# A triangular inverse's second merge level from 32-column products without a mask, and the next k evacuated and convolved ahead of v's last tanh and SiLU

## Time and profile before

| what | value |
|---|---|
| median of 3 runs | 1137.81 us (1136.37 to 1139.96) |
| the profiled execution's own time | 1139.61 us |
| its span, first to last instruction | 1137.9 us |
| TensorE busy | 1072.2 us (94%) |
| VectorE busy | 780.1 us (69%) |
| ScalarE busy | 509.7 us (45%) |
| GpSimd busy | 524.0 us (46%) |
| DMA, share of 16 engines | 27.2% |

### The profile page before, as it was taken

One profiled execution on the slowest core, in us unless ns is written; L12 is line 12 of the kernel. 1 busy time (PEld: TensorE's weight loads), 2 busy tenths in 40 slices (PEclk: granted clock), 3 DMA queues, 4 the chain that ended last, 5 costly groups with the idle time before them and its releaser, 6 DMA issues.

```text
span 1137.9 us, 18866 instructions
## 1 busy us (share of the span) xinstructions
PE 1072.2 (94%) x5372; PEld 876.3 (77%) x5372; DVE 780.1 (69%) x1664; ACT 509.7 (45%) x1262; POOL 524.0 (46%) x753
## 2 busy tenths in 40 slices
PE   3897799999999999999999999999999999999984
PEld 2766588878888888888888888888888888887863
DVE  4678585785858586685858586695758586695835
ACT  3663434444344434444354434435354444435333
POOL 2242544555344643546344653546343653446413
PEclk9898999999999999999999999999999999999988
DMA  9922231223121331223221231223221221213103
GB/s 316 305 87 68 66 78 49 58 57 98 46 66 39 83 77 47 57 58 88 55 66 39 74 84 40 66 58 84 59 60 45 74 73 52 66 58 84 31 28 129
DMA packets 142054, 87.29 MB, mean 77 GB/s; under 512 B 21254, under 2 KB 136616, under 8 KB 141992
## 3 DMA queue, kind: packets, MB, share of 16 engines
q1 hardware_dynamic: 141992, 86.68, 27.2%
HBM read 77.76 MB, written 8.91 MB: 76 GB/s over the span
## 4 chain that ended last, share of the span: by engine, by line
PE 79%; DVE 11%; issue 4%; ACT 2%; DMA 1%; POOL 1%; SPq 0%; DVEq 0%; ACTq 0%; POOLq 0%
PE bank L415 37%; PE bank L517 16%; DVE work L967 3%; PE bank L561 2%; PE bank L549 2%; PE bank L571 2%; PE bank L553 2%; PE bank L574 2%; PE bank L490 2%; DVE y L990 2%; PE bank L599 2%; PE bank L476 1%; PE bank L430 1%; PE bank L463 1%; PE bank L437 1%
## 5 line engine op out<-in xcount | busy, mean ns | idle before, releaser
L1377 POOL TENSOR_TENSOR w_lo<-w_raw,w_hi 128x256 fp32r<-128x256 f32 x384 | 304.9, 825 | 280.2 <-ACT w_hi L696 270.5
L415 PE MATMUL bank<-h_hi,w_hi 128*128 128x512 f32 x760 | 327.4, 431 | 4.6 <-ACT w_hi L696 4.6
L415 PE MATMUL bank<-h_lo,w_hi 128*128 128x512 f32 x760 | 300.6, 396 | 0.0
L415 PE MATMUL bank<-h_hi,w_lo 128*128 128x512 f32 x760 | 203.2, 399 | 0.0
L967 DVE SCALAR_TENSOR_TENSOR work<-pre,cw,work 128x512 f32<-128x512 f32 x192 | 164.2, 855 | 13.3 <-ACT work L723 4.8
L415 PEld LDWEIGHTS bank<-h_hi,w_hi 128*128 128x128 f32 x760 | 144.0, 190 | 34.6 <-ACT w_hi L696 5.3
L415 PEld LDWEIGHTS bank<-h_hi,w_lo 128*128 128x128 f32 x760 | 142.6, 188 | 30.2
L415 PEld LDWEIGHTS bank<-h_lo,w_hi 128*128 128x128 f32 x760 | 144.2, 190 | 27.4 <-issue 0.5
L1420 POOL TENSOR_TENSOR og_lo<-work,og_hi 128x256 fp32r<-128x256 f32 x64 | 47.3, 739 | 217.1 <-ACT og_hi L778 217.1
L737 ACT ACTIVATE work<-work 128x512 f32<-128x512 f32 x64 | 40.3, 629 | 219.1 <-DVE work L967 208.1
L517 PE MATMUL bank<-wo_hi,og_hi 128*128 128x512 f32 x256 | 113.3, 443 | 7.1 <-DVE y L990 7.1
(11 more groups left out here) (175 smaller groups left out, 1745.5 us busy)
## 6 DMA issues: line engine op xcount, KB each, us to landing
w_raw<-in_gdn_w_in SPq DMA_DIRECT2D x96, 512.0 KB, 4.0
work<-in_ada_w SPq DMA_DIRECT2D x8, 1024.0 KB, 9.6
w_raw<-in_gdn_w_out SPq DMA_DIRECT2D x16, 512.0 KB, 3.4
y<-in_x SPq DMA_DIRECT2D x8, 512.0 KB, 9.3
work<-in_ada_w SPq DMA_DIRECT2D x8, 512.0 KB, 5.2
n_dram<-work SPq DMA_DIRECT2D x16, 256.0 KB, 2.3
out<-y SPq DMA_DIRECT2D x8, 512.0 KB, 2.6
work<-in_ada_b SPq DMA_DIRECT2D x1, 512.0 KB, 5.4
```

The costliest lines, as they stand in the source:

```text
L415: mm = nc.tensor.matmul(bank[m % 2][:, :], w[:, m % 2, k, :], h[:, k, half, :], start=(r == 0), stop=(r == MM - 1))
L1377: i = nc.gpsimd.tensor_tensor(w_lo[:, k % 2, j:j + 2, :], w_raw_k[:, k % 2, j:j + 2, :], w_hi[:, k % 2, j:j + 2, :].bitcast(F32), ALU.subt ...
```

## The change

The second merge level (`lv == 1`) takes only the blocks that are wanted. `merge_p` makes, for each chunk and each b in (0, 64), a product of 32 stationary columns against 32 moving ones, written to partitions b+32 to b+64. `merge_p_out` copies that into `pm` with two plain copies of 32 partitions, with no mask; `merge_d` likewise makes two products of 32 by 32 columns per chunk; `merge_d_out` subtracts with two instructions. The mask tile loses its middle level. `turn_k` and `decay_exponents` move from behind level 1 to behind level 2's first product. On ScalarE k's evacuation moves ahead of v's last tanh, and on VectorE v's last SiLU moves behind k's convolution.

```
-        pair_mask = sb("pair_mask", [P, 3, P])
+        pair_mask = sb("pair_mask", [P, 2, P])
...
-                    if lv < 2:
+                    if lv == 0:
                         mm = nc.tensor.matmul(p_bank[:, c, :, :], nmat[:, c, :], pairs(tm, lv)[:, c, :, 0, :],
                                               start=True, stop=True)
+                    elif lv == 1:
+                        for b in (0, 64):
+                            mm = nc.tensor.matmul(bank[5][b + 32:b + 64, DV + c * 32:DV + (c + 1) * 32],
+                                                  nmat[:, c, b + 32:b + 64], tm[:, c, b:b + 32], start=True, stop=True)
...
-                    if lv < 2:
+                    if lv == 0:
                         mm = nc.tensor.matmul(halves(bank[4], lv)[:, c, :, :], pm[:, lv, c, :], u_odd,
                                               start=True, stop=True)
+                    elif lv == 1:
+                        for b in (0, 64):
+                            mm = nc.tensor.matmul(bank[4][b:b + 32, c * 32:(c + 1) * 32], pm[:, lv, c, b:b + 32],
+                                                  u_fin[:, c, b + 32:b + 64], start=True, stop=True)
...
                 for lv in range(3):
                     merge_p(u, lv)
+                    if lv == 2 and not last:
+                        turn_k(u + 1, 1 - par)
+                        decay_exponents(u + 1)
                     fill(in_merge[lv][0])
                     merge_d(u, lv)
                     fill(in_merge[lv][1])
-                    if lv == 1 and not last:
-                        turn_k(u + 1, 1 - par)
-                        decay_exponents(u + 1)
...
+                if not last:
+                    evacuate(u, par, hd + par, 0)
                 tanh(u - 1, 5, 3, cvv[:, 1, :])
...
                 else:
-                    evacuate(u, par, hd + par, 0)
...
+                if lv == 1:
+                    for b in (0, 64):
+                        i = nc.vector.tensor_copy(pm[b + 32:b + 64, lv, :, b:b + 32],
+                                                  bank[5][b + 32:b + 64, DV:DV + NCH * 32].rearrange(
+                                                      "p (c w) -> p c w", c=NCH))
+                    i.then_inc(S["merge_p_out"], 1)
+                    return
...
+                        for b in (0, 64):
+                            u_odd = u_fin[b:b + 32, :, b + 32:b + 64]
+                            i = nc.vector.tensor_tensor(u_odd, u_odd, bank[4][b:b + 32, 0:NCH * 32].rearrange(
+                                "p (c w) -> p c w", c=NCH), ALU.subtract)
...
                 merge_p_out(u, 1)
-                silu(u - 1, 5, cvv[:, 1, :])
                 if first:
                     gate_wo(hd, 0)
                 if not last:
                     conv(u, par, nxt, 0)
+                silu(u - 1, 5, cvv[:, 1, :])
...
-            for lv in range(3):
+            for lv in (0, 2):
```

More of the change, by code:

```diff
@@ L1058, in merge_p_out @@
                 passed(dve, "merge_p", u, lv + 1)
+                if lv == 1:
[5 more added lines that the diff above has]
+                    return
                 p_out = (pairs(pm[:, lv, :, :], lv)[:, :, :, 0, :] if lv < 2
                          else pm_last.rearrange("p c (b w) -> p c b w", w=w))
-                mask = pair_mask[:, lv, :].rearrange("p (b q w) -> p b q w", q=2, w=w)[:, :, 0, :]
+                mask = pair_mask[:, lv // 2, :].rearrange("p (b q w) -> p b q w", q=2, w=w)[:, :, 0, :]
                 nc.vector.tensor_tensor(p_out, halves(bank[5], lv, (lv % 2) * DV),
@@ L1068, in merge_d_out @@
                 if lv < 2:
-                    u_odd = pairs(u_fin, lv)[:, :, :, 1, :]
-                    nc.vector.tensor_tensor(u_odd, u_odd, halves(bank[4], lv), ALU.subtract
-                                            ).then_inc(S["u_merged"], 1)
+                    if lv == 0:
+                        u_odd = pairs(u_fin, lv)[:, :, :, 1, :]
+                        i = nc.vector.tensor_tensor(u_odd, u_odd, halves(bank[4], lv), ALU.subtract)
+                    else:
+                        for b in (0, 64):
+                            u_odd = u_fin[b:b + 32, :, b + 32:b + 64]
+                            i = nc.vector.tensor_tensor(u_odd, u_odd, bank[4][b:b + 32, 0:NCH * 32].rearrange(
+                                "p (c w) -> p c w", c=NCH), ALU.subtract)
+                    i.then_inc(S["u_merged"], 1)
                     passed(dve, "u_merged", u, lv + 1)
@@ L1344, in _ @@
             select(after[:, :], [[-1, P]], -1, 1, ALU.is_ge, 0.0)
-            for lv in range(3):
+            for lv in (0, 2):
                 s = BLK << lv
                 n = P // (2 * s)
-                m = pair_mask[:, lv, :].rearrange("p (b q w) -> p b q w", q=2, w=s)[:, :, 0, :]
+                m = pair_mask[:, lv // 2, :].rearrange("p (b q w) -> p b q w", q=2, w=s)[:, :, 0, :]
                 then(nc.gpsimd.memset(m, 1.0))
```

## The result

| | before | after |
|---|---|---|
| median, us | 1137.92 (4 runs, 1136.37 to 1139.96) | 1124.05 (4 runs, 1122.74 to 1125.45) |
| ratio, 95% interval | | 0.9877 [0.9855, 0.9899] |
| the profiled execution, own time / span | 1139.61 / 1137.9 | 1122.74 / 1120.9 |

The change makes the kernel 13.9 us faster.

What follows compares the result with a forecast made beforehand. TensorE, busy 94% of the span, was taken to bound the kernel, with its waits for VectorE. Blocks -2.2, seven waits -2.9 and unit 0 -0.8 gave -5.9 us: 1132, range 1127 to 1146.5.

Steps and rivals of the forecast that it cites:

- the bounds of the narrow block: Level 1 block on TensorE, before 0.90 us: upper 1.24 (+10.9 in all), lower 0.58 (-10.2), middle 0.83 taken (-2.2).
- Rival C: Level 1's two column groups overlap, 16 instructions costing what 8 do: -13.9 us, 1123.9; chance 0.07.
- rival D: Level 1 blocks: every change of column group pays the fixed 0.33 us again, +74 us, about 1206; chance 0.05.
- A: Level 1 blocks slower: narrow products no faster than 0.057 us each, +7.2 us with the waits, 1145.0; chance 0.15.
- The 1.32 us: Level 1 block priced from the skill page's bound of about 62 ns per matmul; +13 us on these blocks alone.
- The seven waits: Transpose of k waiting 0.42 us for VectorE's SiLU in units 2, 4, ... 14; moving turn_k removes them, -2.9 us.
- the slack of 0.44: Unit 2: level 1's transpose ends 0.44 us before level 2's first product would start, so no wait there.
- same 0.42 us before another line in even units: Sign that the forecast is wrong: even units' 0.42 us wait on TensorE stands before a different line.
- VectorE's two for one: Level 1 on VectorE: two copies and two subtractions replace one each, +0.3 us a unit, at most +0.8.
- Unit 0, -0.8 us: Level 2's first product goes into TensorE's wait for VectorE's chain in unit 0, saving 0.8 us.
- k_gram: ScalarE's exponential stays early enough for k_gram: cover falls from 1.93 to 1.1 us, without a wait.

Runs made afterwards that it cites:

- e3_groups_in_turn: Changed kernel with the same 16 instructions per level 1 block, all of one column group first, then all of the other: 1127.87 us, ratio 0.9921.
- e5_turn_k_only: Changed products with turn_k and decay exponents moved behind level 2's first product, ScalarE and VectorE in the order of the kernel before: 1127.86 us, ratio 0.9916.

## Why the prediction was wrong

**The step that failed is the choice between the bounds of the narrow block.** I took 0.33 + 16 x 0.031 = 0.83 us "since the pace halved exactly when the columns did", -2.2 us in all. Measured is 0.57, the lower bound's 0.58: 0.33 less a block, and 0.33 x 32 = 10.6 us. The pace of one group was right, 0.032 between neighbours in `e3_groups_in_turn`, and so was the fixed 0.33. What I missed is that 16 instructions alternating between two groups are two streams of eight. No row before held two column groups, and I read that as evidence against overlap ("no row shows any overlap of blocks"), where it is none for either side. Rival C had the mechanism and the price of a block and a chance of 0.07. A page that I had read for rival D says it: TensorEngine Tiling of the Trainium skill, section Key Properties, that different tiles can load weights and multiply in parallel. The trace after agrees, with loads 0.015 us apart. I used only that section's sentence on draining. That rival C's sum, 1123.9, is met to 0.2 us is in part luck: it has 2 x 0.32 + 0.42 = 1.06 us in an even unit and 0.64 in an odd one, and the traces have 0.78 and 0.93.

**Rivals A and D.** Both are excluded. The block costs 0.57; A wanted 1.24, D some 2.3 more. The 1.32 us that I had estimated for a block is excluded too. That a change of group doesn't drain the engine is shown by seven changes in a block of 0.57 us.

**The seven waits, -2.9 us.** With the old products this was right: the order alone loses them and gives 5.1 us instead of 3.7. The extra is in two places. 0.14 us an even unit lies between level 1 and the Gram matrix and I can't assign it further. 0.19 an odd unit is a wait that I had not counted, level 0's second product behind VectorE's masked copy. L490's idle time for that copy was 3.3 us in 7 waits before and 1.9 in 6 with the order alone. In the changed kernel it is this, at L494:

```profile
  DVE pm L1078: 1.9, 6
```

In the changed kernel itself the waits did not go but moved. TensorE comes to level 2's first product 0.67 us sooner, and the slack of 0.44 that I had worked out is used up. In an even unit this product starts 0.29 us later behind level 1 than in an odd one, and the transpose of k behind it another 0.19 later, since it still waits for the SiLU: 0.48 us, as much as even units lost before (9.36 - 8.88 in the table, and 8.87 - 8.39 after). That is the "same 0.42 us before another line in even units" of my last sentence. In unit 2 (TensorE, then VectorE):

```profile
246.67 1.98 PE L415 MATMUL bank<-h_hi,w_lo 128*128 128x512 f32 x8
248.88 0.68 PE L483 MATMUL bank<-work 128*64 128x64 f32 x8 [0.23 <-DVE work L1098]
249.68 0.65 PE L424 MATMUL bank<-ident,work 128*128 128x128 f32 x4
```

```profile
242.75 0.59 DVE L1070 COPY pm<-bank 32x128 f32<-32x128 f32 x2
243.37 2.77 DVE L976 SCALAR_TENSOR_TENSOR work<-pre,cw,work 128x512 f32<-128x512 f32 x3
246.06 0.68 DVE L983 SCALAR_TENSOR_TENSOR work<-work 128x512 f32<-128x512 f32 x1
246.66 1.22 DVE L1043 TENSOR_TENSOR w_raw<-w_raw,gate_bc 128x1024 f32<-128x1024 f32 x1
247.91 0.57 DVE L1091 TENSOR_TENSOR work<-work,bank 32x128 f32<-32x128 f32 x2
248.52 0.30 DVE L1098 STREAM_TRANSPOSE work<-work 32x128 f32<-32x128 f32 x1
248.85 0.69 DVE L983 SCALAR_TENSOR_TENSOR work<-work 128x512 f32<-128x512 f32 x1
```

From 242.75 to 248.82 VectorE has no gap to speak of, and L483 starts 0.06 later. The SiLU ends at 249.54 and the transpose of k starts at 249.68, 0.80 behind L483; in unit 5 it is 440.11 - 439.50 = 0.61. The convolution follows the copies at once, as I had said; the earlier trace rows had the wait between.

**The sum as a sum.** I added the blocks and the waits. The two runs of a part each show that they don't add: with the blocks alone all 10.6 us turn into waits for VectorE, since in every unit the time that TensorE can come earlier without waiting (the cover) is shorter than the gain. The move of turn_k puts level 2's first product, about 0.8 us, ahead of it in each unit. `e5_turn_k_only` shows that this move by itself brings back 10.4 us.

**VectorE's two for one.** I took +0.3 us a unit. The copies and the next instruction start 0.62 apart (242.75 to 243.37), the subtractions and the transpose 0.61 (247.91 to 248.52). Before, one masked copy took 0.34 and one subtraction 0.44 from start to start, so it is +0.45 us.

**Unit 0, -0.8 us.** It is 1.13 us shorter with both parts. How much of that is the order can't be told: the products alone make it 0.04 us shorter, at the same granted clock over the unit (0.95), and the trace of the order alone, 0.50 us longer, has it at 0.89. So no run shows the -0.8 by itself. Level 2's first product did go ahead of the transpose of k, but it started only at the end of the wait, 3.77 us of it, when level 1's transpose was done; the SiLU cost another 0.28. The clock over 124 to 128 us was the same as in the earlier trace rows:

```profile
124.00:128.00 4.00, 4.00 (x17) 2.34 (x17) 0.53 (x2) 2.75 (x13) 3.97 (x7) 0.60 0.01 2
```

**k_gram.** No wait came back there. TensorE has no idle time before it in the trace, and from the transpose of k to it are 4.01 us in even and odd units alike.

## What to carry to other kernels

Before adding a saving on the busiest engine to the sum, ask at the next wait on that engine how much earlier it may come; where the other engine's chain is the longer one, the saving is zero, and a piece of independent work moved in between can be worth as much as the saving (10.4 of 10.6 us here). Small products that write different partition groups should be issued alternating between the groups, not group by group: 0.57 against 0.72 us a block here. A row that doesn't hold the case in question is no evidence against either side: the chance should follow the mechanism.

## What the runs showed of the hardware

- Products with 32 stationary columns in different column groups run side by side. Two groups: 16 float32 instructions in a block of 0.57 us, against 0.72 with the groups in turn. Four groups: 32 in 0.57 us with 16 moving columns, and 0.78 with 64.
- The pace of one group follows its stationary columns: 0.112 us an instruction at 128, 0.057 at 64 and 0.032 at 32. With 32 stationary columns the moving ones can set it too: 32 instructions in four groups took 0.78 us with 64 moving columns and 0.57 with 16. Instructions of different groups can start within 0.008 us.
- A block that uses a part of the array costs about 0.33 us beside its products, in and out: 0.35 at 64 columns, 0.30 at 32 rows, and 0.57 - 8 x 0.031 = 0.32 at 32 columns.
- On VectorE two operations on 32 partitions and 128 elements took 0.61 us from the first start to the next instruction's, one on 128 partitions and 256 elements 0.34 to 0.44.
